# Taking three weight units instead of two token tile by token tile where the first block's feed-forward turns into the second block's mixer

## What is computed

```python
# first block, end
h = rmsnorm(x, g_ff_pre)
y = jnp.square(jax.nn.relu(h @ w_ff1)) @ w_ff2      # 4096 -> 1024
x = x + rmsnorm(y, g_ff_post)
# second block, start
h = rms_norm(x, norm_mix_g)
proj = h @ w_in                                     # split into many parts; a_k, a_v are one 512-column group
```

## Time and profile before

| | us |
|---|---|
| median of 3 runs | 921.76 |
| lowest, highest | 921.55, 922.35 |
| the profiled execution | 921.96 |
| its span, first to last instruction | 920.1 |
| TensorE matmul busy in it | 897.4 (98%) |
| VectorE busy | 575.2 (63%) |
| ScalarE busy | 511.8 (56%) |
| POOL busy | 89.6 (10%) |

### The profile page before, as it was taken

One profiled execution on the slowest core, in us unless ns is written; L12 is line 12 of the kernel. 1 busy time (PEld: TensorE's weight loads), 2 busy tenths in 40 slices (PEclk: granted clock), 3 DMA queues, 4 the chain that ended last, 5 costly groups with the idle time before them and its releaser, 6 DMA issues.

```text
span 920.1 us, 14611 instructions
## 1 busy us (share of the span) xinstructions
PE 897.4 (98%) x5672; PEld 797.0 (87%) x5672; DVE 575.2 (63%) x899; ACT 511.8 (56%) x932; POOL 89.6 (10%) x111
## 2 busy tenths in 40 slices
PE   6999999999999999999999999999999999999998
PEld 6998977888899998887778989988899799998886
DVE  5455656664676664445656998889846676665333
ACT  4466666664665554335557668787255465554330
POOL 0010000000000000001000412241152101000000
PEclk9999999999999999999999999999999999999999
DMA  9756333464455566555364544454430456555552
GB/s 341 254 183 230 107 124 108 148 226 92 146 175 184 183 207 185 195 202 195 107 214 138 184 139 141 134 164 157 99 143 1 131 190 184 184 183 183 184 189 84
DMA packets 110395, 152.22 MB, mean 165 GB/s; under 512 B 6752, under 2 KB 68344, under 8 KB 109944
## 3 DMA queue, kind: packets, MB, share of 16 engines
q1 hardware_dynamic: 110328, 151.31, 50.7%
HBM read 147.99 MB, written 3.30 MB: 164 GB/s over the span
## 4 chain that ended last, share of the span: by engine, by line
issue 48%; PE 34%; DVE 9%; ACT 4%; POOL 2%; DVEq 1%; DMA 1%; POOLq 1%; ACTq 0%; SPq 0%
PE acc L455 4%; PE acc L469 4%; PE acc L467 4%; PE acc L468 4%; PE acc L457 4%; PE acc L456 4%; DVE s_w_lo L405 3%; ACT s_w_hi L399 1%; PE acc L495 1%; DVE s_qkvT L1522 1%; PE acc L497 1%; PE acc L496 1%; DMA s_w_raw<-in_w_out 1%; ACT s_relu_i L1445 1%; POOL s_rstd L636 1%
## 5 line engine op out<-in xcount | busy, mean ns | idle before, releaser
L405 DVE TENSOR_TENSOR s_w_lo<-s_w_raw,s_w_hi 128x2048 fp32r<-128x2048 f32 (+1 forms) x198 | 312.2, 1594 | 176.5 <-ACT s_w_hi L399 176.2
L399 ACT ACTIVATE s_w_hi<-s_w_raw 128x2048 fp32r<-128x2048 f32 (+1 forms) x198 | 262.7, 1345 | 148.6 <-PE acc L457 102.3
L467 PE MATMUL acc<-s_h_hi,s_w_hi 128*128 128x256 f32 x800 | 229.1, 286 | 0.8 <-DVE s_h_lo L690 0.8
L469 PE MATMUL acc<-s_h_hi,s_w_lo 128*128 128x256 f32 x800 | 227.3, 284 | 0.0
L468 PE MATMUL acc<-s_h_lo,s_w_hi 128*128 128x256 f32 x800 | 227.3, 284 | 0.0
L467 PEld LDWEIGHTS acc<-s_h_hi,s_w_hi 128*128 128x128 f32 x800 | 154.5, 193 | 1.6 <-issue 1.2
L468 PEld LDWEIGHTS acc<-s_h_lo,s_w_hi 128*128 128x128 f32 x800 | 154.6, 193 | 0.3
L469 PEld LDWEIGHTS acc<-s_h_hi,s_w_lo 128*128 128x128 f32 x800 | 154.4, 193 | 0.0
L457 PE MATMUL acc<-s_w_hi,s_hid_lo 128*128 128x512 f32 x224 | 88.3, 394 | 0.0
L456 PE MATMUL acc<-s_w_lo,s_hid_hi 128*128 128x512 f32 x224 | 87.8, 392 | 0.0
L455 PE MATMUL acc<-s_w_hi,s_hid_hi 128*128 128x512 f32 x224 | 86.9, 388 | 0.0
(11 more groups left out here) (323 smaller groups left out, 1429.1 us busy)
## 6 DMA issues: line engine op xcount, KB each, us to landing
s_w_raw<-in_w_in SPq DMA_DIRECT2D x43, 1024.0 KB, 5.2
s_w_raw<-in_w_ff SPq DMA_DIRECT2D x32, 1024.0 KB, 5.2
s_w_raw<-in_w_mlp_up SPq DMA_DIRECT2D x16, 1024.0 KB, 5.5
s_w_raw<-in_w_mlp_down SPq DMA_DIRECT2D x16, 1024.0 KB, 5.0
s_w_raw<-in_w_out SPq DMA_DIRECT2D x8, 1024.0 KB, 5.1
s_w_raw<-in_w_mk SPq DMA_DIRECT2D x4, 1024.0 KB, 5.4
s_w_raw<-in_w_mv SPq DMA_DIRECT2D x4, 1024.0 KB, 5.0
s_w_raw<-in_w_mq SPq DMA_DIRECT2D x4, 1024.0 KB, 5.0
```

What stands on the lines that cost most here:

```text
L399: act.activation(w_hi[u % SPLIT_SLOTS][:, cs], w_raw[u % RAW_SLOTS][:, cs], ACT.Copy).then_inc(w_hi_done, 4 if q is None else 1)
L405: dve.tensor_tensor(w_lo[u % RAW_SLOTS][:, cs], w_raw[u % RAW_SLOTS][:, cs], w_hi[u % SPLIT_SLOTS][:, cs].bitcast(F32), ALU.subtract).then ...
L467: pe.matmul(o, wh[:, cs], hi[:, k, :], start=k == 0, stop=False)
L469: i = pe.matmul(o, wl[:, cs], hi[:, k, :], start=False, stop=k == KC - 1)
```

## The change

`pair_mm` gets the number of its units (`n_units`). At the end of `ff2` it is called with three units, ff2-13 to ff2-15, and the transposes of x's tile 0 move from ahead of `akv` into the pass of tile 1, ahead of the third chunk of ff2-15. `head_mm` transposes only tile 1. In `turn_act` and `turn_dve` the splits of akv-0 and akv-1 are no longer done early (akv-0) and in quarters (akv-1), but each as a whole unit at a later place, behind halves (four chunks) of the activations of tile 0. The end of the kernel (`down`) keeps its pair.

```diff
-        def pair_mm(pe, u, hi, lo, fresh=None, before_t=None, within=None):
+        def pair_mm(pe, u, hi, lo, fresh=None, before_t=None, within=None, n_units=2):
...
-                for v in (u, u + 1):
+                for v in range(u, u + n_units):
...
-                        if within is not None and (v, kk) == (u + 1, 2):
+                        if within is not None and (v, kk) == (u + n_units - 1, 2):
...
 # turn_act
             post_stats(act, post, tag, 0)
-            advance_hi(act, last - 1)
-            for t in range(NT):
+            for t in range(NT):
+                if t:
+                    nt_tile_act(act, pre, hi, 0, range(4))
                 post_stats(act, post, tag, 1, [t])
                 if t:
-                    nt_tile_act(act, pre, hi, 0, range(4))
-                    for q in (2, 3):
-                        advance_hi(act, last, q)
                     nt_tile_act(act, pre, hi, 0, range(4, KC))
+                    advance_hi(act, last)
                 for g in range(2):
                     act.wait_ge(x_done, 2 * NT * TURN[tag] + 2 * t + g + 1)
                     square(act, pre, g, t, x[:, t, g * 512:(g + 1) * 512])
                 if t == 0:
-                    for q in (0, 1):
-                        advance_hi(act, last, q)
+                    advance_hi(act, last - 1)
...
 # turn_dve
-            advance_lo(dve, last - 1)
             post_gain(dve, post, tag, n_load, 1, 0)
             post_add(dve, post, 0)
             x_dve_scale(dve, pre, 0)
-            for q in (0, 1):
-                advance_lo(dve, last, q)
+            advance_lo(dve, last - 1)
+            nt_tile_dve(dve, pre, hi, lo, 0, range(4))
             post_gain(dve, post, tag, n_load, 1, 1)
-            nt_tile_dve(dve, pre, hi, lo, 0, range(4))
+            nt_tile_dve(dve, pre, hi, lo, 0, range(4, KC))
             post_add(dve, post, 1)
-            for q in (2, 3):
-                advance_lo(dve, last, q)
-            nt_tile_dve(dve, pre, hi, lo, 0, range(4, KC))
+            advance_lo(dve, last)
             x_dve_scale(dve, pre, 1)
             nt_tile_dve(dve, pre, hi, lo, 1, range(KC))
...
 # hidden_mm
+                if tag == "ff2":
+                    pair_mm(pe, of[tag][-3], hid_hi, hid_lo, n_units=3, within=lambda t: nt_tile_pe(pe, xn, 0) if t else None)
+                else:
+                    pair_mm(pe, of[tag][-2], hid_hi, hid_lo)
...
 # head_mm
-                pair_mm(pe, of[tag][0], h_hi, h_lo, normed[0], lambda t: nt_tile_pe(pe, xn, t))
+                pair_mm(pe, of[tag][0], h_hi, h_lo, normed[0], lambda t: nt_tile_pe(pe, xn, t) if t else None)
```

More of the change, by code:

```diff
@@ L2521, in hidden_mm @@
             def hidden_mm(tag):
-                for j in range(len(of[tag]) - 2):
+                n = 3 if tag == "ff2" else 2
+                for j in range(len(of[tag]) - n):
                     if j < len(of[tag]) // 2:
@@ L2525, in hidden_mm @@
                     mm(tag, j, hi=hid_hi, lo=hid_lo)
-                pair_mm(pe, of[tag][-2], hid_hi, hid_lo)
+                if tag == "ff2":
+                    pair_mm(pe, of[tag][-3], hid_hi, hid_lo, n_units=3, within=lambda t: nt_tile_pe(pe, xn, 0) if t else None)
+                else:
+                    pair_mm(pe, of[tag][-2], hid_hi, hid_lo)
             def head_mm(tag):
-                pair_mm(pe, of[tag][0], h_hi, h_lo, normed[0], lambda t: nt_tile_pe(pe, xn, t))
+                pair_mm(pe, of[tag][0], h_hi, h_lo, normed[0], lambda t: nt_tile_pe(pe, xn, t) if t else None)
                 normed[0] += NT * KC
```

## The result

| | before | after |
|---|---|---|
| median, 13 runs each | 922.35 | 924.26 |
| lowest, highest | 921.55, 922.78 | 922.57, 925.40 |
| span of the profiled execution | 920.1 | 920.8 |

The changed kernel is slower: ratio 1.0021, 95% interval 1.0014 to 1.0029, or 1.9 us by the medians. The forecast was +0.68 us, 922.4 within 921.2 to 924.0; the measured median lies 0.26 above that range. Two things differ from what the forecast started from: the median of before rose from 921.76 to 922.35 with more runs, and the difference itself is 1.2 us larger. (One execution of a later run, with quarters, stood at 1105.06 us and a mean clock of 0.755; it is left out of that run's numbers.)

What follows compares the result with a forecast made beforehand. TensorE was taken as the bound, so only its waits counted: 3.35 us go, 3.96 come, one more restart costs 0.07, the clock 0. That sums to +0.68 us on 921.76, so 922.4 us, range 921.2 to 924.0.

Steps and rivals of the forecast that it cites:

- The bound: Whole kernel: TensorE's matmuls busy 98% of the span, so only its waits count; 3.35 us to win at this turn.
- The matmuls and the place of the transposes: ff2's last pass: tile 0 complete 2.75 us earlier, transposes go in unwaited with 0.46 us margin, removing the 1.07 wait.
- The rival in which tile 0's chain misses its place: Inside ff2: scaling 1 us later than computed makes TensorE wait 0.5 us, giving 922.9; chance 4%.
- akv-0: First akv unit after ff2: starts at 433.26, with 0.24 us of wait left in place of 1.34.
- akv-1, the step that decides: Second akv unit: TensorE waits 3.72 us for its whole low part, where it waited 0.94; bounds 3.5 to 4.2.
- The end of the sum: Start of tile 1's transposes: 442.60 against 441.92 before, +0.68 us; scaled x ready by 441.2.
- The clock: TensorE's clock behind the akv-1 wait: loss between 0 and 2.5 us, taken as 0.
- rows 3: TensorE's timeline at the turn before the change; its waits, up to 1.34 us, were taken as harmless to the clock.
- The rival with the low clock: Clock falls in the wait at akv-1, costing 1.5 to 2.5 us on top, giving 924.4; chance 13%.
- the bound from 0 to 2.5: Behind the akv-1 wait: loss if the lower clock came, up to half of 5 us of work, 2.5 us.
- within 0.2%: Whole-kernel outcome "same": time within 1.84 us of before, from 919.9 to 923.6; chance 0.83.
- slower: Whole-kernel outcome: slower than before by more than 0.2%, beyond 923.6 us; chance 0.14.

Runs made afterwards that it cites:

- the tuned one without extra matmuls: Three units as in the changed kernel, both akv units split in quarters, ScalarE and VectorE reordered, no extra matmuls; median 920.87 us, 0.9983 of before.
- the quarters kernel: Changed kernel with akv-1's low part made in four quarters at the same place of VectorE's order; median 922.55 us, 0.9996 of before.
- another with the same length of wait: Changed kernel with 7 extra matmuls, filling half of TensorE's wait for akv-1; median 922.77 us.
- the trace with filled short waits: Akv-1's low part in quarters, its 1.8 us wait left empty, extra matmuls (1 ahead, 3 behind) around tile 1's transposes; median 921.47 us.
- the old orders: Three units with the transposes in the pass, as in the changed kernel, but ScalarE and VectorE in the order of before; median 930.41 us, ratio 1.0089.
- the kernel with the new orders and two units: Kernel before with only the changed kernel's orders of ScalarE and VectorE, still two units tile by tile; median 925.17 us, ratio 1.0037.

## Why the prediction was right, and where it was wrong

**The bound**: right. The time moved with what TensorE waits for at this turn and with its clock behind the wait; no other engine, load or later stage comes in: from tile 1's transposes to the end of the span it is 478.2 us before (920.1 - 441.92), 478.3 after, 478.2 in the second run of the changed kernel and in the tuned one without extra matmuls.

**The matmuls and the place of the transposes**: right. Tile 0's last matmul starts at 423.61 (423.69 expected), the transposes go in at 430.70 without a wait (430.79), and they hold up the pass by 0.80 (0.79). The scaled x was there at 430.29, 0.41 ahead. The rival in which tile 0's chain misses its place did not happen.

**akv-0**: right, 433.21 for 433.26. (The section on the change puts both akv splits behind halves of tile 0's activations. In the kernel only akv-1's stands there; akv-0's whole split stands ahead of the first four chunks on both engines, and the sum has it so.)

**akv-1, the step that decides**: right in kind and size. Expected a start at 439.79 and 3.72 us of wait between starts; measured 439.62 and 439.62 - 436.06 = 3.56 (3.41 in the record, which counts from a modelled end). The chain is the one named, the squares of tile 1, four chunks, the residual and the whole low part.

**The end of the sum**: +0.56 in rows, +0.68 expected. The scaled x of tile 1 was ready at 441.23 (441.2 expected), so it holds nothing up.

**The clock**: this step failed: the term for what the wait at akv-1 does to TensorE's clock, put at 0. It measured 1.65 us in most executions and 2.5 in the others that have it. I wrote that "I take 0, since rows 3, with waits of about 1 us, are the nearer ones". The rival with the low clock, at 13%, gave 924.4; the median is 924.26. Its mechanism, its place and its price (2.0 on top; 1.65 and 2.5 measured in two groups) are what the runs show, and it hits nearly every execution: 11 of 13, then 12 of 12. With 14 extra matmuls in the wait, beside 12 of 12 without them, it hits none of 12. The error was in the weight. Its premise fails too, that the waits of about 1 us in rows 3 (up to 1.34 by the prediction's own sum) are harmless: the kernel before has the lower clock in 30 of 89 executions, and in 0 of 11 with these waits filled. A wait nearly three times as long as any in the rows of the turn has no near row, and the bound from 0 to 2.5 should have been taken at its middle or above. The kernel's start was the only row with a long standstill and work behind it, and it spoke for the loss; I set it aside. The second run of the changed kernel has a granted clock of 1.00 ahead of the wait and 0.57 behind it. The Trainium skill, page TensorE: Matmul & The Clock Gate, Part 1, says that idleness brings the low clock back: this trace agrees.

I also took the one profiled execution, at 1.000, for the kernel before as a whole. A third of its executions have a lower mean clock, which one trace can't tell.

**The chances**: "within 0.2%" had 0.83; the measured ratio, 1.0021, lies just beyond that border, its interval on both sides. The rows' part of the loss, 0.56 us, is inside it, the clock moved it over the edge. The range, up to 924.0, took in only the cheapest end of the clock's case, whose own price of 1.5 to 2.5 gives 923.9 to 924.9. And "slower" had 0.14 where the clock, the one rival that leads there, had 0.13 with a part of it inside 0.2%: these two don't add up.

## What to carry to other kernels

On an engine that is bound by its own work, price a new wait twice: its length, and what the clock does behind it. Several short waits are not the same as one long one of the same sum: here one of 3.4 us cost another 1.65 to 2.5 in 23 of 25 executions, while 0.9, 1.1, 0.75 and 0.5, 3.3 in sum, brought the clock down in 30 of 89 and cost 0.3 to 0.5 where they did; 1.1, 0.6 and 0.5 cost nothing beyond themselves in 11 executions. When a unit of preparation is moved later to clear the way for another chain, keep it in pieces that are signalled one by one: at the same place, quarters made the wait 1.8 us where the whole unit made it 3.4. And where one execution can't tell, look at the list of executions with their clocks before believing the trace.

## What the runs showed of the hardware that I had not expected

- A wait of 1.8 us of TensorE in full work is enough for the 1.2 GHz level in a part of the executions, 8 of 11 in the quarters kernel, 2 of 11 in another with the same length of wait, on another chip. The level can come 1.3 to 1.6 us after the wait, in the middle of gapless matmuls (439.67 in the trace with filled short waits, 444.32 in that of the old orders).
- The column of the granted clock doesn't show every low stretch. At the start of the kernel before it says 1.00 from 11.70 to 16.50 us, where 256-column matmuls start 0.21 apart, against 0.12 from 16.75 on. Look at the distance of starts as well.
- Matmuls whose result nobody reads keep the clock up at no cost where they fit in the wait: 14 of them took the changed kernel from 924.4 to 922.6, 12 in the waits of the kernel before took the share of its executions with a lowered clock from a third to none of 11.
- POOL's short step on a 128x1 tile took 1.35 us instead of 0.30 when it fell beside VectorE's 2.28 us subtraction:

```profile
434.05 0.30 POOL L634 TENSOR_SCALAR s_stat<-s_stat 128x1 f32<-128x1 f32 x1 [4.54 <-ACT s_junk L603]
...
438.38 1.35 POOL L634 TENSOR_SCALAR s_stat<-s_stat 128x1 f32<-128x1 f32 x1 [3.33 <-ACT s_junk L603]
```

In the changed kernel it ended at 439.73, the subtraction at 439.57, with cover to spare. In the tuned one without extra matmuls it took 0.94 and ended at 439.32, the subtraction at 439.15; the scaling waits for it, and TensorE then waits 0.60 for the scaled x, which is about the 0.64 us that the step had lost. The 1.14 in the earlier trace rows is the same again: it ended at 434.38, the subtraction beside it at 434.28.

What stays open: what sets the share of executions in which a wait of 1.8 us brings the clock down, and why the kernel with the new orders and two units lost nothing, and the kernel before less than half a microsecond, to a clock as low as the one that cost the changed kernel 1.65.
